# Retention's group variance as two split passes behind the outer products, a third output bank, and decay masks built in the input projection

## What is computed

```python
scores = jnp.einsum('bhncd,bhnsd->bhncs', qc, kc) * decay_mask[None, :, None]
intra = jnp.einsum('bhncs,bhnse->bhnce', scores, vc)
cross = jnp.einsum('bhncd,nbhde->bhnce', qc * q_decay[None, :, None, :, None], states_prev)
return (intra + cross).reshape(b, h, t, dv)
...
out_f = retention_scan(q, k, v, log_decay[0], state_fwd)
out_b = flip_t(retention_scan(flip_t(q), flip_t(k), flip_t(v), log_decay[1], state_bwd))
...
mu = jnp.mean(of, axis=-1, keepdims=True)
var = jnp.mean(jnp.square(of - mu), axis=-1, keepdims=True)
on = merge_heads((of - mu) * lax.rsqrt(var + EPS)) * gn_w.astype(F32)
return (jax.nn.silu(g.astype(F32)) * on).astype(g.dtype)
```

## Time and profile before

| what | us |
|---|---|
| median of 3 runs (3542.89 to 3551.83) | 3545.27 |
| the profiled execution, whole | 3543.9 |
| its span | 3542.1 |
| TensorE busy | 3404.4 (96%) |
| VectorE busy | 2411.3 (68%) |
| ScalarE busy | 1265.5 (36%) |
| GpSimd busy | 774.3 (22%) |
| retention of layer 0, first part, from 405.1 to 440.6 | 35.5 |
| retention of layer 0, turns, from 440.6 to 484.5 | 43.8 |
| retention of layer 1, first part, from 2265.3 to 2302.3 | 37.0 |
| retention of layer 1, turns, from 2302.3 to 2336.8 | 34.6 |

### The profile page before, as it was taken

How to read it: one execution, slowest core, us unless ns; L and a number is a source line. 1 busy time by engine, 2 the same in 40 slices (tenths; PEclk the granted TensorE clock), 3 DMA queues, 4 the chain that set the end, 5 groups by cost and what they waited for, 6 DMA issues and landing times. The chain is left out here.

```text
span 3542.1 us, 48987 instructions
## 1 busy us (share of the span) xinstructions
PE 3404.4 (96%) x18304; PEld 2882.0 (81%) x18304; DVE 2411.3 (68%) x3535; ACT 1265.5 (36%) x2137; POOL 774.3 (22%) x365
## 2 busy tenths in 40 slices
PE   8999899999989999999998899899999999999996
PEld 4888788888878888888887688789998788888884
DVE  6575567886198999998666543478992665665665
ACT  4332356775231121112113432366772322222222
POOL 1221210001312222222223111310013222222223
PEclk9999999999999999999999999999999999999998
DMA  5455462221122222222110424462112111111111
GB/s 227 153 188 199 127 191 62 54 67 66 30 79 71 71 71 71 71 71 77 37 41 18 167 94 147 144 190 55 55 46 74 43 53 47 42 53 47 41 47 48
DMA packets 95948, 304.22 MB, mean 86 GB/s; under 512 B 11584, under 2 KB 38336, under 8 KB 93632
## 3 DMA queue, kind: packets, MB, share of 16 engines
q1 hardware_dynamic: 95808, 302.33, 26.1%
HBM read 239.11 MB, written 63.18 MB: 85 GB/s over the span
## 5 line engine op out<-in xcount | busy, mean ns | idle before, releaser
L2110 DVE SCALAR_TENSOR_TENSOR xT<-down_acc,mod,xT 128x512 f32<-128x512 f32 (+1 forms) x840 | 541.6, 695 | 188.4 <-PE down_acc L183 185.8
L181 PE MATMUL up_acc<-h_hi,whi 128*128 128x512 f32 (+1 forms) x1720 | 637.9, 371 | 13.3 <-DVE h_lo L466 11.3
L183 PE MATMUL up_acc<-h_hi,wlo 128*128 128x512 f32 (+1 forms) x1720 | 635.3, 369 | 0.0
L182 PE MATMUL up_acc<-h_lo,whi 128*128 128x512 f32 (+1 forms) x1720 | 635.2, 369 | 0.0
L130 POOL TENSOR_TENSOR wlo<-raw,whi 128x1024 fp32r<-128x1024 f32 x133 | 341.3, 2567 | 1147.2 <-ACT whi L119 1147.2
L181 PEld LDWEIGHTS up_acc<-h_hi,whi 128*128 128x128 f32 x1720 | 325.6, 189 | 71.7 <-issue 10.3
L183 PEld LDWEIGHTS up_acc<-h_hi,wlo 128*128 128x128 f32 x1720 | 325.1, 189 | 54.1
L182 PEld LDWEIGHTS up_acc<-h_lo,whi 128*128 128x128 f32 x1720 | 325.4, 189 | 52.8
L2002 ACT ACTIVATE up<-up_acc 128x512 f32<-128x512 f32 (+1 forms) x210 | 115.8, 553 | 610.6 <-PE up_acc L183 610.3
L183 PE MATMUL down_acc<-hid_hi,first_wlo 128*128 128x512 f32 (+1 forms) x840 | 321.4, 383 | 0.0
L181 PE MATMUL down_acc<-hid_hi,first_whi 128*128 128x512 f32 (+1 forms) x840 | 316.6, 377 | 4.0 <-DVE xT L2110 4.0
(11 more groups left out here) (277 smaller groups left out, 6315.2 us busy)
## 6 DMA issues: line engine op xcount, KB each, us to landing
raw<-in_w_rest SPq DMA_DIRECT2D x112, 512.0 KB, 3.5
norm_buf<-in_w_ada SPq DMA_DIRECT2D x52, 768.0 KB, 4.5
first_raw<-in_w_rest SPq DMA_DIRECT2D x57, 512.0 KB, 3.6
proj_scratch<-stage SPq DMA_DIRECT2D x18, 640.0 KB, 4.4
raw<-in_w_first SPq DMA_DIRECT2D x21, 512.0 KB, 6.3
ada_raw<-in_w_ada SPq DMA_DIRECT2D x6, 1536.0 KB, 14.0
xT<-proj_scratch SPq DMA_DIRECT2D x4, 1920.0 KB, 8.6
xT<-in_xT SPq DMA_DIRECT2D x8, 640.0 KB, 24.9
```

What stands on the lines that cost most here:

```text
L181: nc.tensor.matmul(out, hi, xhi, start=start, stop=False)
L182: nc.tensor.matmul(out, hi, xlo, start=False, stop=False)
L183: return nc.tensor.matmul(out, lo, xhi, start=False, stop=stop)
L2110: nc.vector.scalar_tensor_tensor(xs, db[g % DB][:, :w], mod_of(layer, 5, m, c), xs, ALU.mult, ALU.add).then_inc(added, 1)
```

## The change

**Variance.** Each output block is squared by ScalarE into fp32 (`osq`), copied by ScalarE to a rounded fp32r half (`osq_hi`), and VectorE subtracts to get the low half (`low`, `osq_lo`). TensorE multiplies both halves by an fp32r copy of the averaging matrix (`mean_r`, made once per layer by ScalarE), in two fp32r passes in place of one fp32 product. `variance(i-2)` now stands behind `outer(i-1)`. **Third bank.** `po` gets a third bank (`pv_`), and `outer(i)` waits for the output of three turns earlier. **Order.** ScalarE does `log` and `root` last in a turn, behind `square` and `diagonal`; VectorE does `finish` first in a turn, for three turns earlier. **Masks.** The 12 exponentials and the three GpSimd products move to the end of the input projection, in the memory of `cos8` and `sin8`; their tables come by three DMAs at tile 15. The `decq` exponentials move from blocks 6 to 8 to blocks 7 to 9. **Attention.** In the second token block `scores` waits also for the outputs that use the third bank.

```diff
@@ -491,4 +491,4 @@
 
-        n, small = 4 * TOK, {}
-        for name, shape in (("dist", (2, P)), ("keep", (2, P)), ("qpos", (2, P)), ("pos", (RH, 2)), ("lg", (RH, 2)), ("lgp", (3, 2)),
+        n, small = 3 * TOK, {}
+        for name, shape in (("mask", (RH, P)), ("qpos", (2, P)), ("pos", (RH, 2)), ("lg", (RH, 2)), ("lgp", (3, 2)),
                             ("centre", (1, P)), ("mean", (1, P))):
...
@@ -508,2 +508,3 @@
         FARTHER = 2
+        MASKS = 15
         place, n = {}, 0
...
@@ -548,2 +549,7 @@
             arena = xT[:, :, :].rearrange("p k n -> p (k n)")
+            rk, rv, small = ret_views(arena)
+            lg = s.sb("lg", [P, RH, 2])
+            decay = [x[:, 0:RH * P].rearrange("p (h s) -> p h s", s=P) for x in (cos8, sin8)]
+            dist, sides = (x[:, RH * P:SEQ].rearrange("p (d s) -> p d s", s=P) for x in (cos8, sin8))
+            table_in, mask_part, mask_made = s.sem("table_in"), s.sem("mask_part"), s.sem("mask_made")
             cqn = arena[:, 0:2 * TOK].rearrange("p (j n) -> p j n", j=2)
...
@@ -632,2 +638,6 @@
                         keep(f"q{u - 12}", [(mq_d[i, u - 12, :, q0:], x[:, q0:]) for i, x in enumerate((hb, lb))])
+                    if u == MASKS:
+                        sp.wait_ge(roped, rope_at["q2"] + 1)
+                        for dst, src in ((dist, a["ret_dist"]), (sides, a["ret_keep"]), (lg, a["ret_lg"][layer])):
+                            sp.dma_start(dst[:, :, :], src).then_inc(table_in, 16)
                     if u >= RK:
...
@@ -664,2 +672,8 @@
                 ring.los(pool, base + AHEAD, base + NTILE)
+                pool.wait_ge(mask_part, 2 * RH)
+                for d in range(2):
+                    nc.gpsimd.tensor_tensor(decay[d], decay[d], sides[:, d, :].unsqueeze(1).to_broadcast([P, RH, P]), ALU.mult).then_inc(mask_made, 1)
+                pool.wait_ge(mask_made, 2)
+                pool.wait_ge(roped, len(ROPES))
+                nc.gpsimd.tensor_tensor(small["mask"], decay[0], decay[1], ALU.add).then_inc(mask_made, 1)
 
...
@@ -835,2 +849,7 @@
                         high("q2", hb[:, q0:], cqn[:, 0, q0:])
+                    if u in (MASKS, MASKS + 1):
+                        d = u - MASKS
+                        act.wait_ge(table_in, 48)
+                        for h in range(RH):
+                            nc.scalar.activation(decay[d][:, h, :], dist[:, d, :], ACT.Exp, scale=lg[:, h, d:d + 1]).then_inc(mask_part, 1)
 
...
@@ -1111,2 +1130,5 @@
                                 pe.wait_ge(lo_done, cut[n - 2] + p + 1)
+                        if n == heads.index(XB) + 1 and k0 == 4:
+
+                            pe.wait_ge(ret.out_done, ret.turns - ret.turns % 3)
                         if n == heads.index(XB) + 1 and k0 == 8:
...
@@ -1324,8 +1346,10 @@
             bd = s.sb("bd", [P, 2, 3, 2, P])
-            decq = s.sb("decq", [P, 2, 3, P])
-
-            tout = s.sb("tout", [P, 2, 3 * P])
-            osq, rt = s.sb("osq", [P, 2, 3 * P]), s.sb("root", [P, 2, 3 * P])
+            mean_r = s.sb("mean_r", [P, P], f32r)
+            osq, tout = s.sb("osq", [P, 2, 3 * P]), s.sb("tout", [P, 2, 3 * P])
+            rt = s.sb("root", [P, 2, 3 * P])
+            osq_hi, osq_lo = s.sb("osq_hi", [P, 2, 3 * P], f32r), s.sb("osq_lo", [P, 2, 3 * P], f32r)
             gate = s.sb("gate", [P, 2, 3, P])
-            mtmp, mask = s.sb("mtmp", [P, RH, P]), s.sb("mask", [P, RH, P])
+            on = rt
+            mask = small["mask"]
+            decq = s.sb("decq", [P, 2, 3, P])
             dec = s.sb("dec", [P, RH, 2])
...
@@ -1346,3 +1369,3 @@
             pv_, pk = s.ps("pv", [P, 512]), s.ps("pk", [P, 512])
-            po = psum_banks(s, "po", 2)
+            po = psum_banks(s, "po", 2) + [pv_]
             qz_in, head_in = s.sem("qz_in"), s.sem("head_in")
...
@@ -1421,8 +1445,2 @@
                 nc.gpsimd.memset(bd[:, :, :, :, :], 0.0).then_inc(bd_zero, 1)
-                pool.wait_ge(masks_made, 2 * RH)
-                for d, m in ((0, mask), (1, mtmp)):
-                    nc.gpsimd.tensor_tensor(m[:, :, :], m[:, :, :], small["keep"][:, d, :].unsqueeze(1).to_broadcast([P, RH, P]),
-                                            ALU.mult).then_inc(mask_made, 1)
-                pool.wait_ge(mask_made, 2)
-                nc.gpsimd.tensor_tensor(mask[:, :, :], mask[:, :, :], mtmp[:, :, :], ALU.add).then_inc(mask_made, 1)
                 pool.wait_ge(decq_made, 6)
...
@@ -1436,6 +1454,9 @@
             def variance(pe, i):
-                pe.wait_ge(sq_done, i + 1)
+                pe.wait_ge(lo_made, i + 1)
                 if i:
                     pe.wait_ge(logged, i)
-                nc.tensor.matmul(pk[:, :3 * P], og, osq[:, i % 2, :], start=True, stop=True).then_inc(var_done, 1)
+                else:
+                    pe.wait_ge(mean_made, 1)
+                nc.tensor.matmul(pk[:, :3 * P], mean_r[:, :], osq_hi[:, i % 2, :], start=True, stop=False)
+                nc.tensor.matmul(pk[:, :3 * P], mean_r[:, :], osq_lo[:, i % 2, :], start=False, stop=True).then_inc(var_done, 1)
 
...
@@ -1488,6 +1509,6 @@
                     pe.wait_ge(qd_done, 2 * (i + 1))
-                    if i >= 2:
-                        pe.wait_ge(out_done, i - 1)
+                    if i >= 3:
+                        pe.wait_ge(out_done, i - 2)
                     for t in range(3):
-                        dst = po[i % 2][:, t * P:(t + 1) * P]
+                        dst = po[i % 3][:, t * P:(t + 1) * P]
                         for half in range(2):
...
@@ -1505,6 +1526,6 @@
                         inner(i)
-                    if i >= 2:
-                        variance(pe, i - 2)
                     if 1 <= i <= NO:
                         outer(i - 1)
+                    if i >= 2:
+                        variance(pe, i - 2)
 
...
@@ -1526,4 +1547,3 @@
                 nc.scalar.activation(cdec[:, :, :], small["lgp"], ACT.Exp, scale=float(P)).then_inc(dec_made, 1)
-                tables = [(m, d, h) for d, m in ((0, mask), (1, mtmp)) for h in range(RH)]
-                tables += [(decq, d, t) for d in range(2) for t in range(3)]
+                tables = [(d, t) for d in range(2) for t in range(3)]
 
...
@@ -1543,7 +1563,4 @@
                         keep(c - 1)
-                    for dst, d, j in tables[2 * c:2 * c + 2]:
-                        if dst is decq:
-                            nc.scalar.activation(decq[:, d, j, :], small["qpos"][:, d, :], ACT.Exp, scale=small["lgp"][:, j, d:d + 1]).then_inc(decq_made, 1)
-                        else:
-                            nc.scalar.activation(dst[:, j, :], small["dist"][:, d, :], ACT.Exp, scale=small["lg"][:, j, d:d + 1]).then_inc(masks_made, 1)
+                    for d, t in tables[2 * (c - BLK + 3):2 * (c - BLK + 4)] if c >= BLK - 3 else []:
+                        nc.scalar.activation(decq[:, d, t, :], small["qpos"][:, d, :], ACT.Exp, scale=small["lgp"][:, t, d:d + 1]).then_inc(decq_made, 1)
 
...
@@ -1566,11 +1583,13 @@
                     if i >= 2:
+                        act.wait_ge(lo_made, i - 1)
+                    nc.scalar.activation(osq[:, i % 2, :], po[i % 3][:, :3 * P], ACT.Square).then_inc(sq_done, 1)
+                    if i >= 2:
                         act.wait_ge(var_done, i - 1)
-                    nc.scalar.activation(osq[:, i % 2, :], po[i % 2][:, :3 * P], ACT.Square).then_inc(sq_done, 1)
+                    act.wait_ge(sq_done, i + 1)
+                    nc.scalar.activation(osq_hi[:, i % 2, :], osq[:, i % 2, :], ACT.Copy).then_inc(hi_made, 1)
 
                 nc.scalar.preload_act_table_set(LN_EXP)
+                nc.scalar.activation(mean_r[:, :], og, ACT.Copy).then_inc(mean_made, 1)
                 diagonal(0)
                 for i in range(NO + 1):
-                    if i >= 2:
-                        log(act, i - 2)
-                        root(act, i - 2)
                     if 1 <= i <= NO:
...
@@ -1579,2 +1598,5 @@
                         diagonal(i + 1)
+                    if i >= 2:
+                        log(act, i - 2)
+                        root(act, i - 2)
 
...
@@ -1633,4 +1655,2 @@
                     dve.wait_ge(a_done, i + 1)
-                    if i == 0:
-                        dve.wait_ge(mask_made, 3)
                     if i >= 2:
...
@@ -1643,3 +1663,10 @@
                     backward(j)
+                def low(i):
+                    dve.wait_ge(hi_made, i + 1)
+                    if i >= 2:
+                        dve.wait_ge(var_done, i - 1)
+                    nc.vector.tensor_tensor(osq_lo[:, i % 2, :], osq[:, i % 2, :], osq_hi[:, i % 2, :].bitcast(f32), ALU.subtract).then_inc(lo_made, 1)
                 for i in range(NO + 1):
+                    if i >= 3:
+                        finish(dve, i - 3)
                     if i < NO:
...
@@ -1648,4 +1675,5 @@
                         backward(first + i + 1)
-                    if i >= 2:
-                        finish(dve, i - 2)
```

(19 more changed lines are left out.)

13 lines of the change are left out of this document (5 added, 8 removed).

## The result

| | us |
|---|---|
| before, median of 6 (3542.89 to 3551.83) | 3549.53 |
| changed kernel, median of 6 (3557.88 to 3562.35) | 3560.94 |
| ratio, 95% interval | 1.0034 [1.0024, 1.0045] |
| profiled execution of the changed kernel, whole | 3562.35 |

The change costs 11.4 us in the medians (8.5 to 16 by the interval); 6.5 were forecast, and the time lies above the range. Part of the miss is the base: the three runs that were shown had a median of 3545.3, all six have 3549.5. So the traces are compared stage by stage, not by their spans (3542.1 and 3560.5; the execution traced before was 5.6 us faster than its median, and the new one 1.4 slower).

A forecast was written before the change was run, and what follows sets the result against it. TensorE was taken to bound the retention turns, 4.62 us each without gaps; after the change, a ring through ScalarE and VectorE. Layer 0 +3.7 and layer 1 +2.85 gave +6.5: 3551.8 us by the median, range 3541 to 3558.

The forecast's parts named there:

- Masks in the projection: End of the input projection: the moved mask exponentials, DMAs and GpSimd products are hidden beside a busy TensorE; price 0.
- First part: Retention before the turns: without mask products, layer 0 gains 3.85 us and layer 1 gains 2.15.
- The variance: Retention turns: two fp32r passes take 0.35 us against 0.65, making TensorE's own turn 4.32 us.
- The ring: Retention turns: diagonal ahead of log closes a one-turn wait loop through ScalarE and VectorE, 4.99 us bare, 5.55 with GpSimd.
- The meetings with GpSimd: Retention turns: GpSimd's pair delays the state step 0.62 us one turn, "on" 0.48 the next.
- The wait at attention's start: Between retention and attention: the first maximum comes later, costing 2.45 us in layer 0 and 1.7 in layer 1.
- The clock: Rival, in the retention turns: TensorE's clock falls to 1.2 GHz, 3.1 us more a turn; 3583 us; chance 0.06.
- the stated bound: Whole kernel: a difference within 0.3%, 10.6 us, counts as no change; chance of that 0.85.

The follow-up runs named there:

- logarithm first: The changed kernel with ScalarE's log and root put back ahead of the diagonal; 3543.70 us, ratio 0.9983 to the kernel before.
- GpSimd writes: The changed kernel with GpSimd's two decayed-query products per turn replaced by memsets from the third turn on; 3555.83 us, one run.
- filler at the start only: The changed kernel with unread TensorE products filling waits in attention's start alone, none in the turns; 3556.25 us, ratio 1.0020 to the kernel before.
- finish late: The changed kernel with the second-last finish moved behind attention's first maximum on VectorE; 3552.53 us, ratio 1.0010 to the kernel before.
- filler: The changed kernel with unread products in TensorE's waits before outer products and in attention's start, all waits kept; 3553.69 us, ratio 1.0007 to the kernel before.
- before, with a stall: The kernel before with unused VectorE maxima added ahead of attention's first maximum, 5 in layer 0, 4 in layer 1; 3554.51 us, ratio 1.0018.
- both: The changed kernel with log and root ahead of the diagonal and the second-last finish behind attention's first maximum; 3539.33 us, ratio 0.9966 to the kernel before.

## Why the prediction was wrong, step by step

**Masks in the projection: right.** TensorE waits for nothing there, and price 0 stood.

**First part: right.** -3.85 forecast, -4.4 measured in layer 0, where the products `pa` came every 2.34 us and not 2.39. Two runs with the same instructions up to there, "logarithm first" and "GpSimd writes", reached the first outer product at 437.46 and 437.50, so 3.2 and 3.1 earlier: the size is known to about 1 us. Layer 1: -2.15 forecast, -3.4 measured. GpSimd's four products held up four state instructions and not eight:

```profile
2305.74 4.21 POOL L1452 TENSOR_TENSOR qd<-rq_first,decq 128x384 f32<-128x384 f32 x4 [14.77 <-ACT decq L1565]
2305.91 1.04 DVE L1639 TENSOR_TENSOR state<-state,cdec 128x192 f32<-128x192 f32 x1
2306.99 1.04 DVE L1641 TENSOR_TENSOR state<-state,kv 128x192 f32<-128x192 f32 x1
2308.17 0.93 DVE L1639 TENSOR_TENSOR state<-state,cdec 128x192 f32<-128x192 f32 x1
2309.14 1.03 DVE L1641 TENSOR_TENSOR state<-state,kv 128x192 f32<-128x192 f32 x1
2310.31 0.36 DVE L1639 TENSOR_TENSOR state<-state,cdec 128x192 f32<-128x192 f32 x1
...
2312.32 0.68 PE L1516 MATMUL po<-at,vz 128*128 128x128 f32 x4 [2.83 <-DVE at L1658]
```

**The variance: right.** TensorE's own turn is 4.33 for 4.32. The two passes stand 0.26 and 0.18 us apart from what follows them (457.60, 457.86, and the inner product at 458.04), 0.44 together; the outer product before them gives 0.09 of it back. By the count of passes of the Trainium skill, "FP8 and Floating Point Precision", TensorE Precision Notes, a turn was estimated at 4.30; the trace has 0.03 more.

**The ring: right, and sized to 4%.** 4.99 us bare was forecast and 5.17 measured; the difference is the way from the diagonal to the logarithm (456.69 - 455.60 = 1.09 for 0.98) and "on" to output (0.66 for 0.59). The six distances were to be 33.3 and were 33.6 in layer 0; four in layer 1 were to be 22.2 and were 22.3. The meetings with GpSimd alternate as forecast.

**The wait at attention's start: right.** +2.45 and +1.7 forecast, +2.1 and +1.8 measured.

**The clock: this step failed.** The prediction had the clock fall only as a rival, and only in the ring turns, at 3.1 us each and 0.06. It noted that the start of attention "now idles 2.45 us longer" and was already at 0.90, and then priced that start as the wait alone. The ring turns kept a clock of 1.00 (440 to 482 in the first profile above). The rule cited for them, of the Trainium skill, "TensorE: Matmul & The Clock Gate", section "A second HAM failure mode: psum-queue depth-cycling", would have slowed just these turns; this trace does not show it. The clock fell at the places with the longer waits: after TensorE's 1.88 us before the last outer product of layer 0, after 1.70 at the first transposes, and in layer 1 after 2.83 before the first outer product and again after 2.53 at the first transposes. The ten transposes of layer 1 show the last, in the changed kernel and then in the one before:

```profile
2358.66 2.40 PE L1151 MATMUL scores<-ident,probs 128*128 128x128 f32 x10 [2.53 <-ACT probs L1216]
...
2341.58 1.31 PE L1129 MATMUL scores<-ident,probs 128*128 128x128 f32 x10 [0.39 <-ACT probs L1194]
```

The clock did not fall each time. Behind the wait of 1.86 to 1.90 us before a last outer product it fell in four places (layer 0 of the change and of "GpSimd writes", both layers of "filler at the start only") and stayed up in four (layer 1 of the change and of "GpSimd writes", both layers of "finish late"); behind the 2.83 it fell in six traces of seven. What decides which is open. What it cost the change, beyond the waits:

| place | forecast | measured | beyond |
|---|---|---|---|
| layer 0, last outer product and variance | 3.03 | 4.72 | 1.7 |
| layer 0, start of attention | 9.49 | 12.19 | 2.7 |
| layer 1, first distance | 3.97 | 5.69 | 1.7 |
| layer 1, start of attention | 9.52 | 11.70 | 2.2 |

That is 8.3 us, less 1.8 that the first parts gained beyond the forecast: 6.5 on top of the forecast 6.5, and so 13.0 of the stages' 13.4. These are sizes in one pair of executions; by the spread above, up to 2 us at each place can be chance. That the term exists and is of this order is shown: "filler" gave back 7.3 to 9.6 us without shortening a wait, "before, with a stall" made layer 1's start 10.9 us for 9.5 in a kernel that has no ring, and the mean clock of whole executions moved with it in both.

The base has its share in the time, though none in the stages. Counted from 3549.5 in place of 3545.3, the same forecast would be 3556 and its range 3545 to 3562, with 3560.9 inside. So the time fell outside the range by the base and the clock together; the mechanism that was left out of the sum is the clock's. What stays open is the rest of the traces' difference, 5 us (5.9 between layer 0's start and layer 1, 0.9 back at the end): a part is further short stretches at a low clock in attention (680 to 700 and 760 to 780 at 0.91 for 1.00), which came and went between runs with the same attention, and executions of the kernel before alone spread over 11 us (3544.4 to 3555.3 in 23 runs).

The verdict by the stated bound: 0.34% lies just beyond the 0.3% that was to count as no change, and the interval, 0.24% to 0.45%, takes the bound in.

## What to carry to other kernels

When a change moves a wait on an engine that feeds TensorE at the border between two stages, price the wait and then the clock behind it: here a wait of 1.4 to 2.1 us at such a border cost nearly as much again behind it, while waits of 0.6 to 1.5 us in every turn cost their length only. Before two engines' orders are changed, write down who waits for whom through one turn: moving one instruction across the turn's border closed a ring and turned a gain of 6.3 us ("logarithm first") into a loss of 11.4. Run apart the parts that travel in one change: the masks alone were a gain of 0.2%, and the variance made up for itself only with the old order on ScalarE and a late `finish`, by 3.2 us that are not clear of the noise.

## What the runs showed of the hardware

- **A wait can cost twice its length.** In layer 1 of "before, with a stall" a wait longer by 1.38 us made the start behind it 1.41 longer; with layer 0, 3.45 us of waits cost 6.4 in the trace. Products that compute nothing, put into such waits, took 7.3 us off the changed kernel. The length of one wait does not decide alone: in layer 0 of "both" the waits in attention's start are 1.07 and 1.18 us, as long as those of the ring turns, and its products of scores took 0.63 for 0.40 behind them, while in "finish late" the same two waits left them at 0.40 until 494.8.
- **GpSimd's reach.** An instruction of VectorE with both operands in SBUF was held up while a GpSimd product ran: state step 1.03 for 0.36, "on" 1.03 for 0.56, pair `vd` 2.52 for 1.03. The masked product, with an operand in PSUM, took its 0.95 beside GpSimd's pair (447.55 against 447.65 to 449.73). GpSimd's memsets did not hold up "on" (0.56).
- **From fp32 to fp32r on TensorE.** The first fp32r pass of 384 columns behind an fp32 outer product starts 0.26 us before the second, the second 0.18 before what follows, and the outer product is 0.09 shorter than in front of fp32 products.
